# Hybrid decoder trunk on one core: the loops over expert units and middle strips written out on TensorE, ScalarE and VectorE

## The reference

```python
def swiglu(x, w_gate, w_up, w_down):
    return (jax.nn.silu(x @ w_gate) * (x @ w_up)) @ w_down

def moe_swiglu(xn, w_router, we_gate, we_up, we_down):
    logits = (xn @ w_router).astype(jnp.float32)
    top_v, top_i = lax.top_k(logits, TOP_K)
    top_w = jax.nn.softmax(top_v, axis=-1)
    gates = jnp.sum(jax.nn.one_hot(top_i, N_EXPERTS, dtype=jnp.float32) * top_w[..., None], axis=-2)
    y = jnp.zeros_like(xn)
    for e in range(N_EXPERTS):
        y = y + gates[..., e:e + 1].astype(xn.dtype) * swiglu(xn, we_gate[e], we_up[e], we_down[e])
    return y
```

## Time and profile before

| | before |
|---|---|
| median of 3 executions | 1449.0 us (1445.98 to 1450.72) |
| the profiled execution, its own time | 1446.29 us |
| its span, first to last instruction | 1443.4 us |
| TensorE matmul busy | 1410.2 us, 98% |
| VectorE busy | 1192.3 us, 83% |
| ScalarE busy | 1042.5 us, 72% |
| mean granted TensorE clock | 0.994 |
| read from HBM | 433.54 MB, 306 GB/s over the span |

### The profile page before, as it was taken

One profiled execution on the slowest core, in us unless ns is written; L12 is line 12 of the kernel. 1 busy time (PEld: TensorE's weight loads), 2 busy tenths in 40 slices (PEclk: granted clock), 3 DMA queues, 4 the chain that ended last, 5 costly groups with the idle time before them and its releaser, 6 DMA issues.

```text
span 1443.4 us, 20829 instructions
## 1 busy us (share of the span) xinstructions
PE 1410.2 (98%) x6803; PEld 1175.5 (81%) x6803; DVE 1192.3 (83%) x1545; ACT 1042.5 (72%) x1367; POOL 61.8 (4%) x107
## 2 busy tenths in 40 slices
PE   9999999999999999999999979999998999999998
PEld 8998888888888788888888768888877888877886
DVE  6968655545588799899999979889998898999996
ACT  6756544444497677887788868788877788889774
POOL 1000000000010100000010010000010001001000
PEclk9999999999999999999999999999999999999999
DMA  9564555555154699999999999999999999999993
GB/s 313 159 198 162 178 195 176 201 179 178 55 192 148 234 378 382 362 398 375 380 363 404 402 357 354 363 364 401 399 408 354 365 378 352 407 400 397 410 402 145
DMA packets 143071, 442.71 MB, mean 307 GB/s; under 512 B 8862, under 2 KB 20476, under 8 KB 142972
## 3 DMA queue, kind: packets, MB, share of 16 engines
q1 hardware_dynamic: 139772, 429.89, 79.7%
q0 software_dynamic: 3168, 11.54, 2.7%
q10 hardware_dynamic: 32, 0.01, 0.0%
HBM read 433.54 MB, written 7.86 MB: 306 GB/s over the span
## 4 chain that ended last, share of the span: by engine, by line
PE 84%; DVE 9%; issue 4%; ACT 2%; DVEq 0%; POOL 0%; ACTq 0%; POOLq 0%
PE bank L587 80%; DVE w_lo L1946 5%; PE bank L1233 1%; ACT w_hi L1392 1%; DVE qkT L2069 1%; PE bank L932 0%; DVE act_f L2670 0%; PE bank L599 0%; DVE xT_lo L1990 0%; PE bank L607 0%; PE bank L1195 0%; ACT y_out L1895 0%; PE bank L1084 0%; ACT kS L1694 0%; ACT vS L1694 0%
## 5 line engine op out<-in xcount | busy, mean ns | idle before, releaser
L1946 DVE TENSOR_TENSOR w_lo<-raw,w_hi 128x1024 fp32r<-128x1024 f32 (+2 forms) x832 | 956.0, 1196 | 152.1 <-ACT w_hi L1392 143.0
L1392 ACT ACTIVATE w_hi<-raw 128x1024 fp32r<-128x1024 f32 (+2 forms) x832 | 836.9, 1043 | 231.0 <-PE bank L587 209.4
L587 PE MATMUL bank<-w_hi,xT_hi 128*128 128x512 f32 (+3 forms) x1358 | 530.6, 391 | 14.0 <-DVE w_lo L1946 12.1
L587 PE MATMUL bank<-w_hi,xT_lo 128*128 128x512 f32 (+3 forms) x1358 | 523.3, 385 | 0.0
L587 PE MATMUL bank<-w_lo,xT_hi 128*128 128x512 f32 (+3 forms) x1358 | 522.3, 385 | 0.0
L587 PEld LDWEIGHTS bank<-w_hi,xT_hi 128*128 128x128 f32 x1358 | 256.5, 189 | 64.7 <-DVE w_lo L1946 14.7
L587 PEld LDWEIGHTS bank<-w_hi,xT_lo 128*128 128x128 f32 x1358 | 256.4, 189 | 49.7
L587 PEld LDWEIGHTS bank<-w_lo,xT_hi 128*128 128x128 f32 x1358 | 256.9, 189 | 46.6
L587 PE MATMUL bank<-w_hi,aT_hi 128*128 128x512 f32 x544 | 216.0, 397 | 5.4 <-DVE aT_hi L2680 4.7
L587 PE MATMUL bank<-w_lo,aT_hi 128*128 128x512 f32 x544 | 215.0, 395 | 0.0
L587 PE MATMUL bank<-w_hi,aT_lo 128*128 128x512 f32 x376 | 148.7, 396 | 0.0
(11 more groups left out here) (391 smaller groups left out, 750.6 us busy)
## 6 DMA issues: line engine op xcount, KB each, us to landing
raw<-in_we_gate_dram SPq DMA_DIRECT2D x112, 1024.0 KB, 7.8
raw<-in_we_up_dram SPq DMA_DIRECT2D x112, 1024.0 KB, 7.9
raw<-in_we_down_dram SPq DMA_DIRECT2D x112, 1024.0 KB, 8.3
raw<-in_w_gate_dram SPq DMA_DIRECT2D x14, 1024.0 KB, 5.1
raw<-in_w_up_dram SPq DMA_DIRECT2D x14, 1024.0 KB, 5.1
raw<-in_w_down_dram SPq DMA_DIRECT2D x14, 1024.0 KB, 4.9
raw<-in_w_in_dram SPq DMA_DIRECT2D x16, 768.0 KB, 4.5
raw<-in_w_out_dram SPq DMA_DIRECT2D x8, 1024.0 KB, 6.6
```

What stands on the lines that cost most here:

```text
L587: return pe.matmul(o, a, b, start=start, stop=stop, skip_group_check=True, **kw)
L1392: act.activation(split_piece(w_hi, c, shape, half), raw_piece(c, shape, half), ACT.Copy).then_inc(hi_ready, 1)
L1946: dve.tensor_tensor(split_piece(w_lo, c, shape, half), raw_piece(c, shape, half), F(split_piece(w_hi, c, shape, half)), ALU.subtract).then ...
```

## The change

The outer loop over units becomes a Python loop on the three engines, so that seven units are written out one behind the other with constants for the numbers to wait for; so do the inner loops over the middle strips. The instructions that do the work are the same and stand in the same order; SyncE's and GpSimd's code is untouched, and so are the loops of the dense layer (L986, L1650, L2324).

```diff
@@ TensorE
-                with pe.Fori(1, WIDE - 1) as i:
+                for i in range(1, WIDE - 1):
                     e_step(i, False)
...
             start_unit(0, first=True)
-            unit(0)
-            with pe.Fori(0, N_NARROW) as i:
-                unit(2 * i + 1)
-                unit(2 * i + 2, narrow=True)
+            for u in range(NE - 1):
+                unit(u, narrow=u in NARROW_UNITS)
             unit(NE - 1, last=True)
@@ ScalarE
-            def unit(u, n_scattered=0, narrow=False, last=False):
+            def unit(u, narrow=False, last=False):
...
-                with act.Fori(0, WIDE - 1) as i:
+                for i in range(WIDE - 1):
...
-                    act.wait_ge(sem("scattered"), n_scattered)
+                    act.wait_ge(sem("scattered"), scattered_before(u))
...
-            unit(0, scattered_before(0))
-            with act.Fori(0, N_NARROW) as i:
-                unit(2 * i + 1, 48 * i + scattered_before(1))
-                unit(2 * i + 2, 48 * i + scattered_before(2), narrow=True)
+            for u in range(NE - 1):
+                unit(u, narrow=u in NARROW_UNITS)
@@ VectorE
-            def unit(u, narrow=False, first=False, last=False):
+            def unit(u, narrow=False, last=False):
...
-                next_narrow = not narrow and not first
+                first = u == 0
...
-                    mark(u + 1, next_narrow)
+                    mark(u + 1, u + 1 in NARROW_UNITS)
...
-                with dve.Fori(0, WIDE - 1) as i:
+                for i in range(WIDE - 1):
...
-            unit(0, first=True)
-            with dve.Fori(0, N_NARROW) as i:
-                unit(2 * i + 1)
-                unit(2 * i + 2, narrow=True)
+            for u in range(NE - 1):
+                unit(u, narrow=u in NARROW_UNITS)
```

## The result

The changed kernel takes 1427.49 us (median of four runs, 1426.41 to 1429.08), the kernel before 1449.86 us (four runs, 1445.98 to 1452.2): a ratio of 0.9849, 95% interval 0.9825 to 0.9873, 22 us less. Later runs on another occasion gave 1427.51 us for the change beside 1446.65 us for before, a ratio of 0.9864 (0.9848 to 0.9881), 19 us less. The forecast was 1429.0 us within 1424.5 to 1436.0, worked out as 18.8 us less.

What follows compares the result with a forecast made beforehand. TensorE, busy 1410.2 of 1443.4 us, was taken as the bound. 1446.29 - 18.8 = 1427.5 us for the profiled execution, other terms 0; shifting the median gives 1430.2; 1429.0 was taken, range 1424.5 to 1436.

Steps and rivals of the forecast that it cites:

- What bounds, and the comparison of three places: TensorE bounds; between the same two marks behind units 2, 4 (jumps) and 6 (none): 46.78, 44.96 and 36.47 us.
- Outer loops: Behind units 2 and 4, writing out removes two backward jumps on each of three engines: 10.31 + 8.49 = 18.8 us less.
- How the edge comes to cost that: At each jump ScalarE stalls about 5.5 us, then TensorE's branch takes about 6 us; TensorE waits, then runs at half clock.
- Inner loops: Loops over the middle strips: short branches, 42 ns on ScalarE, lie under queued pieces; gain 0, at most 0.3 us.
- Register instructions and longer code: Register work on VectorE is covered by the piece ahead, and written-out code is fetched no more often: 0.
- Rival 4: Straight code's instruction fetching falls behind, with pauses about each 25 us: slower, 1453 us; chance 0.03.
- What is late next: TensorE's waits for turned activations in the narrow units, 4.7 + 2.3 us, stay.
- Rival 2: VectorE's loop overhead causes the narrow units' waits for turned activations, so 7.0 us more goes: 1422 us; chance 0.04.
- rival 3: Something else behind units 2 and 4, the scatter and gather of rows, stops ScalarE; pauses remain: 1449 us; chance 0.04.
- rival 1: Without pauses SyncE's loads reach ScalarE late; 7.6 us lost in unit 3 or 5 gives 1437, both 1444; chance 0.08.

Runs made afterwards that it cites:

- shift by 96: Kernel before with 96 more instructions (waits already met) on ScalarE ahead of the experts: 1453.64 us beside 1447.36 for before.
- the run with 64 instructions: Kernel before with 64 more instructions (waits already met) on ScalarE ahead of the experts: 1436.04 us beside 1447.36 for before.
- the three shifts: Kernel before with 32, 64 or 96 already met waits added on ScalarE ahead of the experts: 1447.56, 1436.04 and 1453.64 us beside 1447.36.
- the short loop: Kernel with all units wide, units 1 to 6 in a hardware loop of one unit a pass: 1460.43 us against 1460.09 written out.
- straight yardstick: Kernel before changed to all units wide (2, 4 and 6 too) and everything written out: 1460.09 us.

## Why the prediction was right

- **What bounds, and the comparison of three places.** Right. The place without a jump, 36.47 us, was the price of straight code to 0.02 us at the two others.
- **Outer loops, -18.8 us.** 18.8 us came back at the two marks of the profiled run. In the medians 22.4 us (first comparison), 18.6 (outer loops alone) and 19.1 us (second comparison) came back. The 22.4 are more than the edges gave: the median before was 1449.86 us there and 1446.65 to 1447.36 on the other occasions. That 1429.0 came within 1.5 us of 1427.49 is in part luck, since the profiled execution, for which the sum said 1427.5, took 1429.08, with a late start of the experts. The profile before wasn't an unlucky one: other executions have edges of 8.5 + 8.7 us (VectorE's loop written out) to 10.2 + 10.0 us (shift by 96).
- **How the edge comes to cost that.** The two stalls in a row and the half clock behind them are shown (one edge of the run with 64 instructions had no half clock): 9.1 us for TensorE's alone, 11.6 us for ScalarE's alone, each with PEclk at 0.96 over the window and 1.00 with neither. TensorE's idle time behind its branch, which the prediction called likely to be the sequencer's, goes with that branch.
- **Inner loops, 0 to 0.3 us.** Right: 938.9 us with these loops, 938.7 without, from the experts' beginning.
- **Register instructions and longer code, 0.** Right. TensorE is busy 109.43 of 109.45 us in the three windows, and its packets of instructions went down, 57 to 52, not up. Rival 4 falls.
- **What is late next.** Right: 7.0 us before and after. Rival 2 falls, as VectorE's loop alone showed too.
- **The branches as the cause (rival 3 denied it).** ScalarE's pause goes with its jump, and goes with a mere shift of the loop, while the scatter and gather stay. Rival 3 falls.
- **The loads (rival 1).** The DMA share rose to 1.03 at 398 GB/s where an edge had been, and TensorE lost nothing.
- **Two rules of the Trainium skill.** The Trainium skill (Runtime: NRT & Kernel Launch, section "Instruction fetch mechanics") says that a taken branch whose target is outside a two-page window forces a fetch of the target. These runs agree: a stall comes with a packet of instructions, and comes or not by distance and by place. The prediction said that VectorE's branch disagreed with it. That was too strong. VectorE's body happened to lie where the target was still held, and when it grew to 443 instructions it stalled as well. The 108 ns for compare-and-branch (the Trainium skill, Advanced Engine Details and Errata, section "Control Flow Timing") lie between what these runs show for a branch without a stall: 34 to 63 ns on ScalarE and VectorE in the experts, 67 on TensorE when it falls through and 209 to 221 when it jumps back over one unit.

Open: how many blocks each engine holds. On TensorE some 1200 instructions back are free and some 2300 aren't; in between nothing was tried. On ScalarE 172 are free and 340 depend on the place. Which places are free was tried at four only, and the three shifts, the short loop and its straight yardstick ran once each; their effects (11 us, a pause there or gone, 1 packet in place of 22) are far beyond the spread. What passes in the 2.2 to 3.9 us between a branch and its packet, and in the 1.6 us behind it, isn't shown.

## What to carry to other kernels

Look at the edges of a hardware loop before writing it out: a jump back is free while its target is still held. When it isn't, it cost 4.4 to 4.7 us an edge on TensorE, the bound here, and 5.8 us on ScalarE, which feeds it; on VectorE, beside the other two, a pause of 2.9 us added nothing. Write out the loop with the long body and keep the short ones, or loop over half the body; register arithmetic beside operations of 1 us was no reason to unroll here. If the code runs once without the jump, the same stretch there gives the gain beforehand. The count of packets on the queues of instructions tells whether a loop's body is held.

## What the runs showed of the hardware that I hadn't expected

- Sixty-four instructions that do nothing, ahead of a loop of 340 on ScalarE, made the kernel 11 us faster. An edit that adds or takes instructions on that engine ahead of such a loop can bring or take 5 us an edge, and would be read as the edit's own effect.
- On TensorE the stall stands in the branch's row (5905 to 6305 ns, and 3442 and 3897 with VectorE's pause ahead of it), on ScalarE and VectorE behind it (45 and 63 ns in the row, then 5.5 and 2.9 us of idle time). The releaser named behind TensorE's is VectorE, though the wait ends 1.6 us behind the packet of instructions.
- It isn't peculiar to jumps back. At the very end TensorE jumps forward over the three units that aren't run, and that branch takes 4283 ns in the kernel before and 4224 ns in the changed one, behind its last matmuls.
- A wait of 2.6 to 4.0 us on TensorE is followed by half clock, which adds 2 us or so: PEclk 0.50 to 0.52. At one edge of the run with 64 instructions it wasn't: behind a wait of 3.06 us PEclk stayed at 1.00, and the edge took 39.81 us in place of 41.55.
- GpSimd's busy time in the first window, most of it the scatter of rows behind a narrow unit, rose from 4.76 us to 18.02. It isn't the loads alone that do it: with the outer loops alone written out, at the same DMA share of 1.03, it is 6.55. The cause is open. Nothing shows in the time: both of these kernels take 36.5 us there.
